# Order of the products in an expert input pass: rounded parts first, low parts last, with a wait for each group

## The reference

```
ue  = u[e]                                   # rows of the input table, one per chosen expert
act = gelu(einsum('td,thkd->thk', h, ue))
ve  = v[e]
out = einsum('thk,thkd->td', g * act, ve)    # g: softmax gate of the chosen experts
```

## Time and profile before

| | us |
|---|---|
| median of 3 runs | 2066.75 (2066.57 to 2066.75) |
| profiled execution, span from first to last instruction | 2076.9 |
| PE busy | 2055.7 (99%) |
| DVE busy | 1530.8 (74%) |
| ACT busy | 1284.6 (62%) |
| share of the chain that ended last: PE | 98% |
| of it the input pass (line 1194) | 35% |

### The profile page before, as it was taken

One profiled execution on the slowest core, in us unless ns is written; L12 is line 12 of the kernel. 1 busy time (PEld: TensorE's weight loads), 2 busy tenths in 40 slices (PEclk: granted clock), 3 DMA queues, 4 the chain that ended last, 5 costly groups with the idle time before them and its releaser, 6 DMA issues.

```text
span 2076.9 us, 40622 instructions
## 1 busy us (share of the span) xinstructions
PE 2055.7 (99%) x15546; PEld 1794.8 (86%) x15546; DVE 1530.8 (74%) x3491; ACT 1284.6 (62%) x2535; POOL 119.9 (6%) x138
## 2 busy tenths in 40 slices
PE   8999999999999999999999999999999999999998
PEld 6776799999999888788887758999999998887887
DVE  5844589868899776576678436998688997766766
ACT  5464445658888665565564544556688886555654
POOL 2200010000000010100022000100000001101000
PEclk9999999999999999999999999999999999999999
DMA  9443437776666888898763543577766668888886
GB/s 313 154 150 143 163 126 254 248 253 221 216 215 214 286 304 296 303 319 279 253 226 141 170 170 116 180 253 250 246 221 209 220 214 300 311 290 295 266 269 220
DMA packets 137376, 481.76 MB, mean 232 GB/s; under 512 B 25666, under 2 KB 42082, under 8 KB 130768
## 3 DMA queue, kind: packets, MB, share of 16 engines
q1 hardware_dynamic: 124640, 438.45, 62.6%
q0 software_dynamic: 10496, 40.42, 5.6%
q10 hardware_dynamic: 2048, 0.30, 0.1%
HBM read 475.83 MB, written 104.21 MB: 279 GB/s over the span
## 4 chain that ended last, share of the span: by engine, by line
PE 98%; DVE 1%; ACT 1%; DMA 0%; issue 0%; DVEq 0%; ACTq 0%
PE ps L1194 35%; PE ps L1241 33%; PE ps L827 4%; PE ps L875 4%; PE ps L919 3%; PE ps L1206 3%; PE ps L1157 2%; PE ps L927 2%; PE ps L1165 1%; PE ps L1161 1%; PE ps L884 1%; PE ps L1016 1%; PE ps L1180 1%; PE ps L1019 1%; PE ps L978 1%; PE ps L1032 1%
## 5 line engine op out<-in xcount | busy, mean ns | idle before, releaser
L2165 DVE TENSOR_TENSOR parts<-region,parts 128x1024 fp32r<-128x1024 f32 x512 | 625.6, 1222 | 300.6 <-ACT parts L1509 298.0
L1194 PE MATMUL ps<-tokens_hi,parts 128*128 128x256 f32 x4096 | 760.5, 284 | 0.0
L1509 ACT CAST parts<-region 128x1024 fp32r<-128x1024 f32 x512 | 538.8, 1052 | 271.0 <-PE ps L1241 221.2
L1241 PE MATMUL ps<-parts,parts_hw 128*128 128x512 f32 x3024 | 688.7, 389 | 0.0
L1241 PEld LDWEIGHTS ps<-parts,parts_hw 128*128 128x128 f32 x3024 | 566.8, 188 | 124.0 <-DVE parts_hw L2215 6.9
L1194 PEld LDWEIGHTS ps<-tokens_hi,parts 128*128 128x128 f32 x4096 | 636.6, 188 | 1.0 <-issue 0.8
L1194 PE MATMUL ps<-parts_hw,parts 128*128 128x256 f32 x2048 | 573.7, 280 | 0.0
L1194 PEld LDWEIGHTS ps<-parts_hw,parts 128*128 128x128 f32 x2048 | 386.5, 189 | 0.0
L1555 ACT ACTIVATE big<-ps 128x256 f32<-128x256 f32 (+31 forms) x252 | 131.7, 523 | 146.9 <-PE ps L1194 146.8
L1543 ACT CAST parts_hw<-big 128x256 fp32r<-128x256 f32 x256 | 170.9, 668 | 0.7 <-DVE big L2226 0.7
L1536 ACT ACTIVATE region<-region 128x128 f16<-128x128 f16 x512 | 169.2, 436 | 0.0
(11 more groups left out here) (316 smaller groups left out, 2172.9 us busy)
## 6 DMA issues: line engine op xcount, KB each, us to landing
region<-in_peer_uT SPq DMA_DIRECT2D x256, 512.0 KB, 4.1
region<-in_peer_v SPq DMA_DIRECT2D x256, 512.0 KB, 4.7
out<-in_state_win_k SPq DMA_DIRECT2D x112, 384.0 KB
out<-in_state_win_v SPq DMA_DIRECT2D x112, 384.0 KB
big<-in_window_keysT SPq DMA_DIRECT2D x16, 576.0 KB, 3.8
big<-in_state_win_v SPq DMA_DIRECT2D x48, 192.0 KB, 4.2
region<-in_w_out SPq DMA_DIRECT2D x4, 2048.0 KB, 8.2
big<-in_peer_wq SPq DMA_DIRECT2D x4, 2048.0 KB, 13.7
```

Source lines behind the costliest of these rows:

```text
L1194: mm = pe.matmul(ps[:, j % ZB, 0:SEQ], a, hp[b][:, c, :], start=(c == 0 and n == 0), stop=(c == KD - 1 and n == 2))
L1241: mm = pe.matmul(ps[:, 2 * half + t, :], w_t[a][:, 128 * t:128 * t + 128], v_t[b][:, 512 * half:512 * half + 512], start=(j == 0 and n == ...
L1509: act.copy(hi_t[n % HIGHS], rows_t[n % ROWS]).then_inc(high[l], 1)
L2165: dve.tensor_tensor(lo_t[n % ROWS], rows_t[n % ROWS], hi_t[n % HIGHS], ALU.subtract).then_inc(low[l], 1)
```

## The change

In `z_of(j)` the 24 products are put in another order. The sixteen that have the rounded part of the `u` tile as weights come first, chunk by chunk, behind a wait for `high[l]`. The eight with the low part as weights come last, behind the wait for `low[l]`, which stood ahead of all 24 before. The products themselves, their count, their weight loads, the bank that they add to and the count-up of `z_prod` at the last of them stay.

```diff
                 def z_of(j):
                     if j >= ZB:
                         pe.wait_ge(gelu_done, j - ZB + 1)
+                    pe.wait_ge(high[l], j + 1)
+                    for c in range(KD):
+                        u_hi = hi_t[j % HIGHS][:, 128 * c:128 * c + 128]
+                        for b in range(2):
+                            pe.matmul(ps[:, j % ZB, 0:SEQ], u_hi, hp[b][:, c, :], start=(c == 0 and b == 0), stop=False)
                     pe.wait_ge(low[l], j + 1)
                     for c in range(KD):
-                        u_hi, u_lo = (p[:, 128 * c:128 * c + 128] for p in (hi_t[j % HIGHS], lo_t[j % ROWS]))
-                        for n, (a, b) in enumerate(((u_hi, 0), (u_hi, 1), (u_lo, 0))):
-                            mm = pe.matmul(ps[:, j % ZB, 0:SEQ], a, hp[b][:, c, :], start=(c == 0 and n == 0), stop=(c == KD - 1 and n == 2))
+                        u_lo = lo_t[j % ROWS][:, 128 * c:128 * c + 128]
+                        mm = pe.matmul(ps[:, j % ZB, 0:SEQ], u_lo, hp[0][:, c, :], start=False, stop=(c == KD - 1))
                     mm.then_inc(z_prod, 1)
```

## The result

| | before | after |
|---|---|---|
| median of 6 runs each (before: the three above and three more) | 2066.75 us (2066.57 to 2074.39) | 2080.24 us (2072.19 to 2080.63) |
| profiled execution, span | 2076.9 us | 2070.3 us (2072.19 us as a run, 1.9 above the span) |
| PE busy | 2055.7 us | 2051.6 us |

A forecast was written before the change was run, and what follows sets the result against it. PE, busy for 99% of the span, was taken to bound the kernel. Removed, added and moved summed to −0.44 + 0 + 0 us, so 2066.75 us became 2066.3 us, with a range of 2062.5 to 2069.7 us.

The forecast's parts named there:

- Removed: Input pass: PE no longer waits for the low part ahead of all 24 products of a tile; −0.44 us.
- the two stalls: Input pass: PE's wait for DVE's low part at tile 11, felt once in each layer, 0.22 us each.
- the one ahead of tile 37: Input pass: 0.23 us idle after tile 36's small products, said to be untouched by the change.
- the idle time: Input pass: idle time of the weight loads, forecast to fall from 1.0 to about 0.5 us.
- Added: Input pass: one wait inside each tile, 256 in all, carried by a weight load or hidden by PE's queue; 0.
- The rival of the broken stream: Input pass: PE doesn't issue past the inner wait, so each tile pays at least 51 ns; 2079.4 us, chance 0.03.
- Moved, "the order": Input pass: 24 products in the new order still take 118.4 ns each, 2.84 us a tile; 0.
- the bound of +1.4 us for the eight: Input pass: only the eight low products at the query_low streak price of 119.1 ns; +1.4 us.
- the outer one of +4.3 us: Input pass, dearer-order rival: all products at 119.1 ns, 2070.6 us; chance 0.04 for beyond 4.1 us.
- The sign by which the text said it would be seen: Input pass: undisturbed tiles at 2.82 or 2.86 us with PE as gapless as before would show the order has a price.
- The sum: Whole kernel: −0.44 + 0 + 0 = −0.44 us, giving 2066.3 us in the runs and 2076.5 us in the profiled execution.
- the range: Whole kernel: the likeliest case's 2064.3 to 2067.7 us, widened to 2062.5 and 2069.7 us.

The follow-up runs named there:

- the wait alone: Kernel before with its old product order, but the low part's wait moved to the first product that needs it; median 2074.2 us, ratio 1.0006.
- its control: The kernel before run again without an edit; median 2072.76 us over 11 runs, ratio 1.0001.
- the order alone: Changed kernel with one wait, for the low part, ahead of all 24 products; median 2079.2 us, ratio 1.0027.
- the shortest pass: Changed kernel with the 32-byte shift and the tokens' chunks 1,088 instead of 1,056 bytes apart; 2072.81 us over 12 runs, ratio 1.0011.
- the old order behind the shift: Old product order with tensors 32 bytes further on: ratio 1.0003; also with chunks 1,088 bytes apart and the wait inside the tile: ratio 1.0.

## Why the prediction was wrong

**Removed: right.** −0.44 us was forecast for the two stalls. The wait alone shortens a pass by 0.21 us, −0.42 us in both. The stall at tile 11 is gone, the one ahead of tile 37 remains with 0.23 us, and the idle time falls to 0.7 us instead of about 0.5, since the trace counts only 0.15 us of idle time for each stall.

**Added: right.** 0 was forecast. 248 waiting instructions stay 248, no idle time stands before the low products, and the wait alone costs a pass nothing that shows. Tile 11's low part is there at 310.88, 1.9 us ahead of its seventeenth product (310.85 + 1.90 = 312.75), where 1.8 was forecast. The rival of the broken stream falls with this.

**Moved, "the order": this step failed.** "I take 118.4 ns for all, that is 0." It is 2.0 + 0.2 = 2.2 us a pass, +4.4 us in all: 17 ns a tile in the mean, or 2.2 ns for each of the eight low products if it is put on these alone. That is past the bound of +1.4 us for the eight and as much as the outer one of +4.3 us, which was given 0.04 as a rival. Two choices led there. The bounds were made from the query's streaks by where their *weights* lie, and the runs show that the tokens' sequence and distance count and the weights' order doesn't (their place was not tried); that the outer bound came out near the measurement is chance. And only plain tiles were looked at: those with gates behind them pay 23 ns each, the larger part. The sign by which the text said it would be seen did come: tiles off 2.84 us with PE as gapless as before. The Trainium skill's fixed addition of 2.5 ns to a matmul ("Wait — 56ns, not 53.3ns?" on the same page), by which no order has a price, doesn't hold here: the same 24 products of 256 columns took from 2.837 to 2.860 us, and two of the orders took more than one of these times.

**The sum: a second failure, in the range.** It was built round three runs that agreed within 0.18 us. Later runs with such times stood at a clock of 0.999; others of the same kernel reach 2075.3. The profile had said so: its execution had a span 10.15 us above the runs, which the text carried along without asking what it was. With the 1.9 us that lie around a span it took an estimated 2078.8 us, 12 us more than the three runs. The stretches at half clock above are a part of that and not all: the kernel before once more, at the same mean clock of 0.995, has a span of 2072.9 us, 4.0 us shorter. Half of these 4.0 us stand in the first 30 us, where the loads of line 927 begin later, in the first profile and then once more:

```profile
28.29 0.19 PEld L927 LDWEIGHTS ps<-input_low,tokens_hi 128*128 128x128 f32 x1 [0.22 <-issue]
```

```profile
26.22 2.97 PEld L927 LDWEIGHTS ps<-input_low,tokens_hi 128*128 128x128 f32 x16 [0.22 <-DVE input_low L1708]
```

Of the 13.5 us between the first two medians some 4.0 are the passes; the other 9.5 go with the clock of the executions drawn, as six runs of before at 2066.6 to 2074.4 stood beside six of after of which five were at 0.994 to 0.996. Repeated, the medians are 2078.3 − 2074.04 = 4.3 us apart, which the passes account for.

**What stays open.** What inside the chip sets the price of a sequence was not found: it hangs on the order of the streamed chunks and on their distance, not on a shift by 32 bytes nor on the order of the weights, and one order can have two paces. All the tile times in the table lie whole multiples of 3.3 ns apart, which no run explains. Whether the change alters how often the clock falls is open too: 3 of 18 runs of the changed kernel reached 0.998 and none 0.999, while of the kernel before 3 of 34, 6 of 23 and 5 of 17 runs reached 0.999, and 0 of 11 in its control. None of the 22 runs of the order alone and of the shortest pass reached 0.999, and 5 of the 24 in the old order behind the shift did.

## What to carry to other kernels

A stream of products without gaps isn't a stream of constant price, and not even one order has one price: where nothing shows the new order on these operands, a cost in either direction deserves more than a small chance, and stretches with other work between them are to be read apart. When the edit is confined to a stage, compare the length of that stage: it repeated to 0.04 us here where the time spread over 9. And a few runs that agree don't bound the time: a profiled execution that stands far above them has something to tell, and the granted clock is the first place to look.

## What was not expected of the hardware

Back-to-back products of the same shapes differ in price by the sequence in which their streaming operand is read: turning round the tokens of 8 in 24 products is worth 1.12 us per 3,072 products (401.01 to 399.89 us), turning round their weights 0.00, and 32 bytes more between two chunks (1,088 instead of 1,056, and the shift that costs nothing) saves 2.78 us in one order and adds 0.23 in the other. The same order settles at 2.840 us a tile in one stretch and at 2.860 in another of the same execution. And on one core alone, the clock of a stretch can stand at 1.00 in one execution and at 0.50 in another of the same program (the changed kernel, 185 to 190 us); it cost 4.4 us in one layer where that could be read, and the times of one kernel spread over 9 us in 2,070.
